# Rows of the expert down projection fetched as neighbouring pairs, and the gate and up columns read with a step of two

## What is computed

```python
for e in range(N_EXPERTS):                      # 8
    gu = xt @ w_gu[e]                           # 1024 x 5632, float32
    g, u = gu[..., :D_FF_EXPERT], gu[..., D_FF_EXPERT:]
    y = y + combine[:, e:e + 1] * ((jax.nn.silu(g) * u) @ w_down[e])   # 2816 x 1024
```

## Time and profile before

| | |
|---|---|
| median of three runs | 1171.66 us (1171.53 to 1172.48) |
| the profiled execution, its own time | 1171.78 us |
| its span, first to last instruction | 1169.7 us |
| mean granted clock of PE | 0.985 |
| PE busy | 1119.3 us, 96% of the span |
| DVE, ACT, POOL busy | 299.0, 224.3, 9.4 us |
| read from HBM | 341.15 MB |

### The profile page before, as it was taken

One profiled execution on the slowest core, in us unless ns is written; L12 is line 12 of the kernel. 1 busy time (PEld: TensorE's weight loads), 2 busy tenths in 40 slices (PEclk: granted clock), 3 DMA queues, 4 the chain that ended last, 5 costly groups with the idle time before them and its releaser, 6 DMA issues.

```text
span 1169.7 us, 21411 instructions
## 1 busy us (share of the span) xinstructions
PE 1119.3 (96%) x9605; PEld 617.1 (53%) x9606; DVE 299.0 (26%) x527; ACT 224.3 (19%) x350; POOL 9.4 (1%) x53
## 2 busy tenths in 40 slices
PE   7887999999999899999999999999999999999968
PEld 5556999998588455343334343353344343353426
DVE  4664544453323524000100100100100100100143
ACT  2352444443222612000000000000000000000033
POOL 3000000000000000000000000000000000000000
PEclk9978999999999999999999999999999999999999
DMA  9805556654142308599999999999999999999950
GB/s 332 291 1 180 181 182 192 201 179 147 36 181 73 144 1 323 191 405 420 417 418 407 410 418 419 417 418 420 414 400 328 417 419 419 417 419 419 417 241 36
DMA packets 114025, 343.63 MB, mean 294 GB/s; under 512 B 7757, under 2 KB 30858, under 8 KB 113930
## 3 DMA queue, kind: packets, MB, share of 16 engines
q1 hardware_dynamic: 113930, 342.22, 74.7%
HBM read 341.15 MB, written 1.05 MB: 293 GB/s over the span
## 4 chain that ended last, share of the span: by engine, by line
PE 91%; DVE 3%; DMA 2%; ACT 1%; SPq 1%; issue 1%; DVEq 0%; ACTq 0%
PE ps L1813 34%; PE ps L1864 12%; PE ps L1563 6%; PE ps L1564 6%; PE ps L1565 6%; PE ps L1547 6%; PE ps L1869 4%; PE ps L1794 3%; PE ps L1683 2%; DMA wring<-in_w_exp_down 2%; PE ps L1837 1%; SPq L378 1%; PE ps L1882 1%; PE ps L1438 1%; PE ps L1460 1%
## 5 line engine op out<-in xcount | busy, mean ns | idle before, releaser
L1813 PE MATMUL ps<-wring,xg 128*32 128x512 f32 (+1 forms) x4704 | 416.3, 502 | 1.5 <-DVE e_h L1286 1.5
L1813 PEld LDWEIGHTS ps<-wring,xg 128*32 128x32 f32 x4704 | 155.6, 110 | 242.2 <-issue 198.1
L1864 PE MATMUL ps<-wring,ehT 128*32 128x512 f32 x1408 | 164.6, 594 | 4.8 <-DMA wring<-in_w_exp_down 4.2
L1563 PE MATMUL ps<-dn_high,w_high 128*128 128x256 f32 x352 | 100.7, 286 | 2.5 <-DVE dn_low L1106 2.5
L1564 PE MATMUL ps<-dn_low,w_high 128*128 128x256 f32 x352 | 100.5, 286 | 0.0
L1565 PE MATMUL ps<-dn_high,w_low 128*128 128x256 f32 x352 | 100.4, 285 | 0.0
L1864 PEld LDWEIGHTS ps<-wring,ehT 128*32 128x32 f32 x1408 | 43.7, 110 | 103.9 <-issue 92.7
L1097 DVE TENSOR_TENSOR w_low<-ring,w_high 128x2048 fp32r<-128x2048 f32 x33 | 75.5, 2292 | 58.3 <-ACT w_high L685 58.3
L802 ACT COPY ehT<-ps 128x384 f32<-128x384 f32 (+1 forms) x24 | 10.5, 439 | 379.3 <-PE ps L1837 266.0
L1298 DVE COPY ehT<-ps 128x384 f32<-128x384 f32 (+3 forms) x24 | 10.8, 450 | 261.9 <-PE ps L1837 192.7
L1563 PEld LDWEIGHTS ps<-dn_high,w_high 128*128 128x128 f32 x352 | 68.5, 195 | 3.3 <-DVE dn_low L1106 2.9
(11 more groups left out here) (288 smaller groups left out, 961.0 us busy)
## 6 DMA issues: line engine op xcount, KB each, us to landing
wring<-in_w_exp_gu SPq DMA_DIRECT2D x128, 1024.0 KB, 16.6
wring<-in_w_exp_down SPq DMA_DIRECT2D x88, 1024.0 KB, 15.6
wring<-in_w_exp_gu SPq DMA_DIRECT2D x64, 768.0 KB, 14.1
ring<-in_w_ffn_gu SPq DMA_DIRECT2D x44, 512.0 KB, 5.0
ring<-in_w_ffn_down SPq DMA_DIRECT2D x11, 1024.0 KB, 4.9
ring<-in_w_ple_gate SPq DMA_DIRECT2D x4, 1024.0 KB, 4.8
ring<-in_w_q_b SPq DMA_DIRECT2D x4, 1024.0 KB, 5.1
ring<-in_w_o_b SPq DMA_DIRECT2D x4, 1024.0 KB, 6.1
```

What stands on the lines that cost most here:

```text
L1563: pe.matmul(out, high_l, high_r, start=first, stop=False)
L1813: return pe.matmul(ps[32 * quarter:32 * quarter + 32, bank, c0:c0 + 2 * nf * P], xg[:, k, 32 * b:32 * b + 32], w[:, :, f * P:(f + nf) * P] ...
L1864: ins = pe.matmul(ps[32 * q:32 * q + 32, 3, :], turned(g, 2 * u + r, b, nb), w[:, r, half * 512:(half + 1) * 512], start=(g == 0 and u == ...
```

## The change

Down: a unit's 256 rows were laid out block by block, partition p getting rows p and 128 + p of the unit (two pieces of 4 KB from places 512 KB apart). Now it gets rows 2p and 2p + 1, which are neighbours in HBM: one piece of 8 KB. Its `w[:, r, ...]` is then row 2p + r.

So that the hidden channels meet these rows, `part` takes, for its block f, not 128 neighbouring columns, but every other column of the pair of blocks that f belongs to: the even ones for even f, the odd ones for odd f. Block f's output column n is channel 2n + f % 2 of the pair. The moving operand has a step of two numbers (8 bytes), its output is written to the same place as before without gaps. The number of instructions, of columns and of bytes stays.

```diff
         else:
             w = a["w_exp_down"][0, bass.ds(e, 1)].rearrange("e k n -> (e k) n")
-            src = rows(w, f0 + 2 * i, f0 + 2 * i + 2)
+            src = w[(f0 + 2 * i) * P:(f0 + 2 * i + 2) * P, :].rearrange("(p s) n -> p s n", s=2)
         sp_.dma_start(unit_at(kind, name, g, i), src).then_inc(landed[unit_no[name, g, i]], 16)
...
                 def part(quarter, b, f, nf, bank, c0, start):
-                    return pe.matmul(ps[32 * quarter:32 * quarter + 32, bank, c0:c0 + 2 * nf * P], xg[:, k, 32 * b:32 * b + 32],
-                                     w[:, :, f * P:(f + nf) * P], start=start, stop=last, skip_group_check=True)
+                    pair = w[:, :, f // 2 * 2 * P:(f // 2 + 1) * 2 * P].rearrange("p s (n r) -> p s r n", r=2)
+                    return pe.matmul(ps[32 * quarter:32 * quarter + 32, bank, c0:c0 + 2 * nf * P].rearrange("p (s r n) -> p s r n", s=2, r=nf),
+                                     xg[:, k, 32 * b:32 * b + 32], pair[:, :, f % 2:f % 2 + nf, :], start=start, stop=last, skip_group_check=True)
```

## The result

The changed kernel takes 1189.05 us (median of four, 1186.65 to 1189.13) against 1171.6 us before: the ratio is 1.0143, with a 95% interval of 1.0126 to 1.0161. It is slower by about 17 us, outside the range of the prediction. The profiled executions differ by 1189.13 - 1171.78 = 17.35 us. Two of the signs of a wrong forecast that the prediction names have come: a longer L1813 (here L1814), and no wait at the down products.

A forecast was written before the change was run, and what follows sets the result against it. PE was taken to set the pace to 1110 us, the DMA queue's last byte the end. Down transfers -0.9 us, gate and up products zero, the rest nothing: 1170.8 us from the median of 1171.66, range 1168.3 to 1174.0.

The forecast's parts named there:

- a longer L1813: Sign of a wrong forecast: gate and up products at L1813 busy for longer than 416 us.
- no wait at the down products: Sign of a wrong forecast: no wait at L1864, which would mean that PE bounds the end.
- What bounds the kernel: Two stages: PE sets the pace to 1110 us; the DMA queue's last byte sets the end of the experts.
- the cap of 5.4 us: At the experts' end: the most that faster transfers could give before PE's own pace bounds the down units.
- The down transfers: Down weights in 8 KB pieces: 1.1% faster, counting for 33 units at the end, 0.9 us gained (0 to 1.8).
- The gate and up products: Products at L1813 reading with a step of two: taken as zero cost, bounds zero and +416 us.
- the rival with 11%: Stepped read slows every L1813 product: p percent longer costs 4.16 us * p, less the tail's give-back; chance 11%.
- the prediction's middle case: Gate and up products: 8.5 bytes a ns is a limit, so some 9% longer, +37 us, 1208 us.
- The second argument: Gate and up products: four plain streams read side by side without hindering each other, 110 ns an instruction.
- The page's rule: Gate and up products: two consecutive accesses in a 16-byte line keep full rate, so step two costs zero.
- The rest: ACT's SiLU, DVE's product, turns, copies and waits: unchanged, costed at nothing.
- its 58%: Chance of the forecast as reckoned: a gain of 0 to 1.8 us, with the stepped read at zero cost.

The follow-up runs named there:

- the kernel with the step alone: Kernel before, with only gate and up products read with a step of two, down rows fetched as before: 1188.49 us, ratio 1.0154.
- the kernel with the rows alone: Kernel before, with only the down rows fetched as neighbouring pairs in 8 KB pieces, no step: 1169.97 us, ratio 0.9993.

## Why the prediction was wrong

**What bounds the kernel** held: PE paces to the end of the gate and up products, the transfers end last. Everything a slower PE did follows from it, with the cap of 5.4 us paid back (5.5 measured).

**The down transfers** held in size: 102,666 packets; 424 GB/s where the kernel after carries down units (1120 to 1140 us) against 419 in the kernel with the step alone:

```profile
1120.00:1140.00 20.00, 20.00 (x280) 10.40 (x272) 2.15 (x5) 2.54 (x5) 0.00 (x0) 1.00 1.02 424
```

```profile
1120.00:1140.00 20.00, 20.00 (x279) 9.40 (x272) 3.87 (x6) 4.82 (x7) 0.00 (x0) 1.00 1.03 419
```

That is 1.2% for 1.1% reckoned. In the kernel with the rows alone the stretch 1109 to 1123 us, nearly all 8 KB pieces, has 422 GB/s against 418, 0.9%, and the gain is 0.8 us for 0.9. The windows move by as much as a GB/s or two, so "about 1%" is what is shown.

**The gate and up products** failed: "I take zero: it is nearest to the row that shows the same rate of bytes." The term is 23.6 us. The bounds (0 and 416 us) held it and the rival with 11% described it, with p = 5.7% where it decides from 0.8%: 23.7 - 5.4 + 1170.8 is 1189.1. What was wrong is the reading of the earlier trace rows: it doesn't show the same rate. The stepped read was reckoned to need 9.3 bytes a ns, the row shows 8.5; so it spoke for the prediction's middle case, in which that rate is a limit, and not for zero. That case was priced too high by rounding: 90 of the 95 distances between the last gate's products in the trace of before are 226 or 227 ns (the row's 0.24 us is one of the others), and L1547 starts every 429 ns. These give 2048 / 227 = 9.02 and 4096 / 429 = 9.55 bytes a ns, a quotient of 1.058, and 5.8% of 416.3 us is 24 us, where 23.6 were measured. So the price stood in the traces of before. The unit is another one, though: step 8, and rounded float32 at step 4 (461 ns), pass over about 18 bytes a ns, and runs of four shifted by two numbers cost 451 instead of 429. For float32 it is lines that are counted, and up to step 4 both counts give the same; rounded float32 follows neither.

The second argument, four streams side by side without loss, was sound (the limit is each stream's own) but beside the point. And the slope was steep around the value I chose: the float32 read needs 429 ns for its columns and 451 for its lines, so a plain read lies just under the limit and the smallest step lies over it.

**The page's rule** was taken as support and shouldn't have been. "SBUF — State Buffer" of the Trainium skill says in the note on cachelines (section "Door 1: The DMA port swizzle") that two accesses in a 16-byte line suffice for the full rate. The kernels here agree on the 16-byte line (fours two numbers later: 451 instead of 429) and disagree on the threshold: at step 2, two accesses a line cost float32 5% and rounded float32 a factor of two.

**The rest** was put at nothing. It held but for the 1.5 us of idle time before the last turn, which go the other way.

**The chances.** Slower had 0.18. Where the one row beside the operation is of another form (another number format, no step), and each percent costs 4.16 us, zero deserved less than its 58%, and the range should have reached the 9% that the prediction itself names.

## What to carry to other kernels

Before a layout is changed for the DMAs' sake, price the engine that reads it: here 88 transfers got about 1% faster, which counts for 33 of them at the end of the kernel, and 4704 products 5.7% slower all through it. If a permutation is needed, put it where few elements pass and an engine has slack (here DVE's product), not into the moving operand of the products that pace the kernel. A row of the trace prices an operation only in its own form. Where a row of another form is all there is and the new operation needs more than the rate it shows (here 9.3 against 8.5 bytes a ns), that is a case to price and not a reason for zero.

## What the runs showed of the hardware

- Moving operand in float32, 512 columns an instruction: 429 ns without a step, 451, 676, 903 and 918 ns at steps 2, 3, 4 and 8; up to step 4 that is 1.76 ns for each 16-byte line (256, 384 and 512 lines), with 429 as the floor. The same alone on the array (429, 451, 900) as with four at once.
- Where the lines lie counts: four of every eight numbers take 429 ns from a multiple of four and 451 two numbers later.
- Rounded float32: 227 ns for whole aligned fours, and 431 to 470 ns for every other pattern tried (steps 2, 3, 4 and 8, pairs, fours two later).
- Weight loads of 128 float32 columns with a step of two take 208 instead of 141 ns.
- Quarters of the array run on their own: a stream that is slower falls behind by itself (some 483 ns an instruction) while the others keep 429, and the lag is paid where all four are needed. This is one run.
- 8 KB pieces move about 1% faster than 4 KB pieces in a full queue (422 to 424 against 418 to 419 GB/s).
